# A two-role decoder step on eight cores: second-half cores split their columns 579 + 512, and 12 tokens change sides

## The reference, cut to what matters

```python
h = rmsnorm(x, g_pre1) * (1.0 + scale1) + shift1
z = h @ w_in                                  # 2048 -> 7168
u_pool, u_lru, g_pool, g_lru = split(z)       # 1024, 2048, 2048, 2048
y_pool = pool_mix(u_pool)                     # causal means over 2/4/8/16 tokens, then per-group maps
xc = causal_dwconv(u_lru, width 4)
y_lru = rglru(xc)                             # per-block gates, then a recurrence over the tokens
merged = sigmoid(g_pool) * (y_pool @ w_pool_up) + sigmoid(g_lru) * (y_lru @ w_lru_up)
x = x + gate1 * rmsnorm(merged @ w_out, g_post1)
h = rmsnorm(x, g_pre2) * (1.0 + scale2) + shift2
upc = causal_dwconv(h @ w_ffn_up, width 3)    # 2048 -> 2 x 6144
f = gelu(gt) * val                            # gt, val: the two parts of upc
x = x + gate2 * rmsnorm(f @ w_ffn_down, g_post2)
```

## Time and profile before

| | |
|---|---|
| runs, median | 2374.85 us (2374.43 to 2376.0, 3 runs) |
| the profiled execution | 2376.36 us |
| its slowest core, span from first to last instruction | 2374.8 us (core 1) |
| spans of all cores | 2292.6 to 2374.8 us |
| busy on core 1: PE / DVE / ACT / POOL | 90% / 44% / 38% / 6% |
| matmuls on core 1 | 17,232 |
| HBM read and written by core 1 | 585.81 MB, 21.32 MB |

### The profile page before, as it was taken

One profiled execution on the slowest core, in us unless ns is written; L12 is line 12 of the kernel. 1 busy time (PEld: TensorE's weight loads), 2 busy tenths in 40 slices (PEclk: granted clock), 3 DMA queues, 4 the chain that ended last, 5 costly groups with the idle time before them and its releaser, 6 DMA issues.

```text
span 2374.8 us, 42702 instructions; the slowest of 8 cores (2292.6 to 2374.8 us)
## 1 busy us (share of the span) xinstructions
PE 2147.8 (90%) x17232; PEld 1076.3 (45%) x17232; DVE 1033.4 (44%) x2122; ACT 899.6 (38%) x1232; POOL 146.5 (6%) x281
## 2 busy tenths in 40 slices
PE   0438988987899999999899999999999999999995
PEld 0124444443455545554345555555554555555552
DVE  0346888897411111110346656550005766553003
ACT  1547787886300000002364454440104444442101
POOL 0000000000000000000000000000000000000000
PEclk9969999999999999999999999999999999999998
DMA  7996575556365556569889988778788997788973
GB/s 170 254 210 107 85 119 90 112 93 125 58 113 110 108 108 113 99 100 181 204 162 196 185 143 142 139 139 172 135 132 154 212 180 135 139 142 187 193 135 94
DMA packets 64908, 336.83 MB, mean 142 GB/s; under 512 B 7360, under 2 KB 7872, under 8 KB 32192
## 3 DMA queue, kind: packets, MB, share of 16 engines
q0 software_dynamic: 39888, 273.17, 66.0%
q1 hardware_dynamic: 24816, 60.83, 7.9%
HBM read 585.81 MB, written 21.32 MB: 256 GB/s over the span
## 4 chain that ended last, share of the span: by engine, by line
PE 85%; ACT 5%; DVE 3%; DMA 2%; issue 2%; another core or an unknown queue 2%; SPq 0%; ACTq 0%; DVEq 0%; POOL 0%; POOLq 0%
PE ps_all L264 85%; ACT sb_R L241 4%; DVE sb_R L244 3%; DMA sb_R<-xp 1%; DMA sb_w<-w_in 1%; ACT L241 1%; DVE sb_R L247 1%; DMA sb_w<-w_ada 0%; SPq L279 0%; DVE sb_mod L254 0%; ACT sb_rstd L241 0%; ACT sb_wsm L241 0%; SPq L404 0%; ACTq L163 0%
## 5 line engine op out<-in xcount | busy, mean ns | idle before, releaser
L264 PE MATMUL ps_all<-sb_R,sb_w 128*128 128x512 bf16 (+4 forms) x14848 | 1976.4, 291 | 19.8 <-DMA sb_w<-w_in 13.2
L264 PEld LDWEIGHTS ps_all<-sb_R,sb_w 128*128 128x128 bf16 x14848 | 976.0, 96 | 1002.1 <-issue 36.3
L241 ACT ACTIVATE sb_R<-ps_all 128x128 f32<-128x128 f32 (+6 forms) x416 | 207.8, 532 | 634.4 <-PE ps_all L264 584.7
L247 DVE SCALAR_TENSOR_TENSOR sb_R<-sb_R,sb_cvec 128x423 f32<-128x423 f32 (+3 forms) x576 | 371.4, 692 | 32.7 <-ACT sb_R L241 21.8
L241 ACT ACTIVATE sb_R<-sb_R 128x551 f32<-128x551 f32 (+9 forms) x216 | 203.5, 963 | 89.9 <-DMA sb_R<-xp 50.1
L244 DVE TENSOR_TENSOR sb_R<-sb_R 128x552 bf16<-128x552 f32 (+9 forms) x148 | 161.5, 1091 | 162.7 <-ACT sb_R L241 148.4
L241 ACT ACTIVATE sb_wsm<-ps_all 128x552 bf16<-128x552 f32 (+1 forms) x64 | 40.4, 632 | 417.5 <-PE ps_all L264 417.2
L241 ACT ACTIVATE sb_R<-ps_all,sb_cvec 128x552 f32<-128x552 f32 (+4 forms) x184 | 166.4, 906 | 18.8 <-DVE sb_R L244 12.8
L244 DVE TENSOR_TENSOR sb_R<-sb_R,sb_mod 128x128 f32<-128x128 f32 x96 | 27.0, 291 | 292.0 <-ACT sb_R L241 288.2
L264 PE MATMUL ps_all<-sb_R,sb_ones 128*128 128x512 bf16 (+2 forms) x160 | 45.2, 403 | 114.1 <-ACT sb_R L241 114.0
L264 PE MATMUL ps_all<-sb_R,sb_wsm 128*128 128x512 bf16 (+2 forms) x432 | 88.5, 350 | 42.3 <-ACT sb_R L241 37.4
(11 more groups left out here) (48 smaller groups left out, 709.3 us busy)
## 6 DMA issues: line engine op xcount, KB each, us to landing
sb_w<-w_ffn_up POOLq DMA_DIRECT2D x96, 1024.0 KB, 10.9
sb_w<-w_ada POOLq DMA_DIRECT2D x48, 1024.0 KB, 13.1
sb_w<-w_ffn_down POOLq DMA_DIRECT2D x48, 1024.0 KB, 9.6
sb_w<-w_in POOLq DMA_DIRECT2D x36, 1024.0 KB, 10.2
sb_w<-w_out POOLq DMA_DIRECT2D x16, 1024.0 KB, 11.6
sb_R<-xm SPq DMA_DIRECT2D x4, 2206.0 KB, 58.6
sb_R<-xp SPq DMA_DIRECT2D x4, 2146.0 KB, 60.0
sb_w<-w_lru_up POOLq DMA_DIRECT2D x8, 1024.0 KB, 12.9
```

Of the source, the lines that this page charges most:

```text
L241: return self.P.op("act", lambda e: e.activation(out=out, in_=in_, func=func, **kw), after)
L247: return self.P.op("dve", lambda e: e.scalar_tensor_tensor(out=out, in0=in0, scalar=scalar, in1=in1, op0=op0, op1=op1), after)
L264: return self.P.op("pe", lambda e: e.matmul(out, lhsT=lhsT, rhs=rhs, start=start, stop=stop), after, signal)
```

## The change

The boundary between the two roles moves by 12 tokens: even cores own 1088 and have N = 1216 columns, odd cores own 960 and have N = 1091, and NP = 1085. On odd cores half B has exactly 512 columns and only one group, and half A has 579, groups of 512 and 67. Even cores have halves of 608 and 608. The longer rows need room: the buffer R grows by 704 bytes a partition, `invc` gives up its own 256 bytes and moves into the scale factors of the first normalization, which are dead by then; it is loaded in `pool_first`, and on even cores only. The merged tensor's place is now above the staging buffers instead of above half B's activations. The signal of a finished block in `ffn_down` moves from the second group's matmul to the last group's.

```diff
@@ -18,14 +18,14 @@
 ENGS = ("pe", "act", "dve", "pool", "sp")
 
 SEQ = 2048
-T0 = 1076
+T0 = 1088
 NSAMP = 128
 SEQS = 16
 TS = 8
 OWNS = (T0, SEQ - T0)
 NMAX = T0 + NSAMP
 NP = T0 - 3
-R_BYTES = 155392
+R_BYTES = 156096
 
 CV_GPRE1, CV_GPOST1, CV_GPRE2, CV_GPOST2 = 0, 16, 32, 48
 CV_PSCALE = 64
@@ -60,8 +60,8 @@
     N = NPR + NSAMP
     SN = (N + 1) // 2 * 2
     SNB = up64(2 * N) // 2
-    NA = (N + 1) // 2
-    NB = N - NA
+    NB = 512 if role else N // 2
+    NA = N - NB
     SB_ = (NA + 1) // 2 * 2
     SBB = up64(2 * NA) // 2
     SPF = (NP + 1) // 2 * 2
@@ -85,13 +85,13 @@
     O_PS = O_PU + 4 * 4 * PU
     O_GB = O_AG
     O_GB3 = O_YPOOL - 4 * SN
-    O_MERGED = O_U
     O_OA = 0
     O_OB = 16 * 4 * SB_
     O_H2A = up64(2 * 16 * 4 * SB_)
     O_H2B = O_H2A + 16 * 2 * SBB
     NXST = 6
     O_XST = O_H2B + 2 * 2 * SBB
+    O_MERGED = max(O_U, up64(O_XST + NXST * 4 * SB_))
     O_FLO = R_BYTES - 32 * 2 * SBB
     O_FHI = 0
     FU = 2 + max(NA, NPR - NA + 160)
@@ -107,7 +107,7 @@
     assert O_SQ + 2 * 2 * SNB <= R_BYTES and O_XCB + 4 * 2 * SNB <= R_BYTES
     assert O_MERGED + 16 * 2 * SNB <= R_BYTES
     assert O_DB + 2 * 2 * SNB <= O_GB3 and O_PS + 2 * 4 * PU <= R_BYTES
-    assert O_GB + 2 * 4 * SN <= O_GB3 and O_H2B + 16 * 2 * SBB <= O_MERGED
+    assert O_GB + 2 * 4 * SN <= O_GB3
     assert O_XST + NXST * 4 * SB_ <= O_H2B + 16 * 2 * SBB <= O_FLO
     assert O_X1ST + 2 * 4 * SB_ <= O_H2B and O_X1B + 16 * 4 * SB_ <= O_FLO
     assert O_FU0 + (2 * (FU + SB_) + 2 * FU + SB_) * 4 <= O_OB
@@ -359,7 +359,6 @@
             self.cvec = self.sb("cvec", [128, NV], F32)
             self.dv = self.sb("dv", [128, 4, 16], F32)
             self.mod = self.sb("mod", [128, 6, 16, 17], F32)
-            self.invc = self.sb("invc", [128, 4, 16], F32)
             self.sl = self.sb("sl", [128, DK, 17], BF16)
             self.hist_lru = self.sb("hist_lru", [128, 16, 3], F32)
             self.h_carry = self.sb("h_carry", [128, 16], F32)
@@ -368,6 +367,7 @@
             self.stl = self.sb("stl", [128, 16, SEQS, 3], F32)
             self.sth = self.sb("sth", [128, 16, SEQS], F32)
             mod0 = self.mod[:, 0].rearrange("p k j -> p (k j)")
+            self.invc = self.mod[:, 1].rearrange("p k j -> p (k j)")[:, 0:64].rearrange("p (g t) -> p g t", g=4)
             self.hist_pool = mod0[:, 0:120].rearrange("p (c t) -> p c t", c=8)
             self.h15 = mod0[:, 120:248].bitcast(BF16).rearrange("p (k t) -> p k t", k=16)
             self.hist_up = self.sth[:].rearrange("p c s -> p (c s)")[:, 0:192].rearrange("p (c t) -> p c t", t=2)
@@ -469,7 +469,6 @@
                 for q in range(4)]
         self.t_stl = self.ld(self.stl[:], self.st_lconv, "stl")
         self.t_sth = self.ld(self.sth[:], self.st_lh, "sth")
-        self.t_inv = self.ld(self.invc[:], self.invc_d, "invc")
         t_one = self.Vset(self.ones[:], 1.0)
         self.t_mod = [None] * 6
         ta = self.A(th, cT, AF.Tanh, scale=0.5, after=[t_c])
@@ -880,6 +879,7 @@
         y_pool = self.bfv(O_YPOOL, 8, SNB)
         self.y_pool = y_pool
         t_stp = self.ld(stp, self.st_pool, "stp", after=half_free)
+        t_inv = None if ROLE else self.ld(self.invc, self.invc_d, "invc", after=half_free)
         groups = [(0, 512), (512, 1024), (1024, N)]
         ring = Ring([0, 3])
         z = {}
@@ -957,7 +957,7 @@
                 dt += [t1, t2]
                 s_done[:] = [t1, t2]
                 if ROLE == 0:
-                    tf = self.Vtt(self.fix[:, c, :], src[:, m0:m0 + 16], self.invc[:, g, :], ALU.mult, t + [self.t_inv])
+                    tf = self.Vtt(self.fix[:, c, :], src[:, m0:m0 + 16], self.invc[:, g, :], ALU.mult, t + [t_inv])
                     t3 = self.Vtt(db[:, c, 0:16], self.fix[:, c, :], u[:, m0:m0 + 16], ALU.subtract, [tf, t1])
                     dt.append(t3)
                 h1 = self.A(self.hist_pool[:, ch, :], u[:, PR - 15:PR], AF.Copy, after=ev[c])
@@ -1074,7 +1074,7 @@
         halves = {
             "A": dict(c0=0, n=NA, npr=NA, groups=[(0, 512), (512, NA)], o=self.f32v(O_OA, 16, SB_),
                       h2=self.bfv(O_H2A, 16, SBB), halo=HALO, y0=0, t_g=[None] * DK, t_d=[None] * DK),
-            "B": dict(c0=NA, n=NB, npr=NPR - NA, groups=[(0, 512), (512, NB)], o=self.f32v(O_OB, 16, SB_),
+            "B": dict(c0=NA, n=NB, npr=NPR - NA, groups=[(0, 512), (512, NB)][:2 - ROLE], o=self.f32v(O_OB, 16, SB_),
                       h2=self.bfv(O_H2B, 16, SBB), halo=0, y0=NA - HALO, t_g=[None] * DK, t_d=[None] * DK),
         }
         f_lo = self.bfv(O_FLO, 32, SBB)
@@ -1330,7 +1330,7 @@
                             first, fin = kk == 0, kk == 47
                             for gi, (a0, a1) in enumerate(H["groups"]):
                                 dd = [wt, ft[kk]] + (self.bfree(bs[j], 2) if first and gi == 0 else [])
-                                sig = k == DK - 1 and gi == 1
+                                sig = k == DK - 1 and gi == len(H["groups"]) - 1
                                 t = self.MM(self.ap_ps(bs[j], a1 - a0, a0), wsl[:, k, j * 128:(j + 1) * 128],
                                             f_ap(kk)[:, a0:a1], first, fin, dd, sig)
                                 if sig:
```

## The result

The changed kernel takes 2340.1 and 2340.4 us, against 2374.4 to 2376.0 before: a ratio of 0.9853, 95% interval 0.9829 to 0.9877. It is faster by 1.5%, and 23 us slower than forecast. The profiled execution took 2340.07 us.

A forecast was written before the change was run, and what follows sets the result against it. TensorE's matmuls were taken to bound the slowest, odd cores: terms summing to -58.9 us took core 1 from 2374.8 to 2315.9, while +20.8 took even core 4 to 2316.9, hence 2317 us, range 2311 to 2331.

The forecast's parts named there:

- (a): Odd cores' second half loses its whole small matmul: 2,608 of 39 columns at 25.3 ns, 66.0 us off.
- (b): Odd cores' first-half small matmul grows from 40 to 67 columns, 25.3 to 30.7 ns: 14.1 us on.
- (c): Odd cores, third group of the main pass: 79 to 67 columns in 1,376 matmuls, 6.9 us off.
- (d): Odd cores, third group of the pass over earlier tokens: 49 to 61 columns in 336 matmuls, 1.0 us on.
- rival 2: FFN matmuls: without the small matmul between, each lone 512 shows its 96 ns weight load; 2566 us, chance 0.03.
- the cover of the finish: Odd cores' second up-projection: stored first-half blocks land in 12.7 us, within two steps of 6.9; no transfer cost charged.
- rival 1: Odd cores' second up-projection: transfers bind at 238 GB/s asked for, through weight tiles or the double buffer; 2321 to 2340 us, chance 0.15.
- The even cores: Wider halves and third groups, last stage and front add 20.8 us, taking core 4 from 2296.1 to 2316.9 us.
- (f): Odd cores' last stage: 16 VectorE operations shrink from 1.31 to 1.22 us each, 1.5 us off.
- (g): Odd cores, loading and normalizing: earlier tokens grow by 1.1%, main ones shrink; 0.7 us on, between 0 and 1.5.
- The sum without the stall: Slowest core is the larger of odd core 1's 2315.9 and even core 4's 2316.9 us, forecast as 2317.

## Why the prediction was wrong

- **Terms (a) to (d)** held: the lone 512, the 67 and the 61 columns measure 215.8, 30.7 to 30.9 and 28.4 ns. The rule of the Trainium skill ("TensorE: Matmul & The Clock Gate", "The mechanism") that weight loads overlap with matmuls in flight only when their row groups differ, and with it **rival 2**, does not hold for this kernel: a 512 behind a 512 with other weights costs 215.8 ns, so nothing of the 96 ns load shows. The prediction left out that the same section also lets a load into a background weight buffer be pulled ahead, which would agree.
- **The step that failed** is the cover of the finish: the sum charges nothing for transfers in the second up-projection, because "TensorE never waited" and 12.7 us to land fit two steps of 6.9, and rival 1 got 0.15. The runs showed in its place a stall of 22.2 us on core 3, out of the 25.0 by which it missed its forecast (33.9 us saved, 58.9 forecast). I had read the waits of core 1 alone, the slowest core, where VectorE waited 2.2 us for stored blocks. Cores 3 and 5 of the same execution, in the same stretch, show the cover already used up:

```profile
DVE sb_R L244 <- DMA sb_R<-x1s: 20.1, 7, 6.0
```

```profile
DVE sb_R L244 <- DMA sb_R<-x1s: 16.6, 7, 6.0
```

  It was 21.7 us on core 7. With three of four odd cores already losing up to 6.0 us at a time, 14% more bytes per us were unlikely to stay hidden, and rival 1 deserved far more than 0.15. Its own text named the place, the double buffer, and the time 2340 at its upper end; the other half of it, late weight tiles, didn't come: TensorE never waited for one. The second error was to hold a median of 12.7 us, again core 1's, against a deadline of 13.8. The same loads took 14.2, 14.1 and 13.5 us in the median on cores 3, 5 and 7 before, so two of the three medians were already past it, and the loads that stop an engine are the late ones, 18 and 21 us on core 3 after the change.
- **The price of the stall** was also cut short: a wait of TensorE of some 5 us costs its length and then a stretch at half clock, 4.5 us on top of 16.9 on core 3.
- **The even cores** were charged 20.8 us and took 12 to 17 more. 6 columns at 1.7 in place of 2.5 ns account for 5,216 x 0.8 = 4.2 us of that; the rest, 0 to 5 us, differs from core to core and was not traced.
- **Term (f)** was small: the 16 operations went from 1.31 to 1.22 or 1.23 us each as forecast, but the whole end behind the last squares only from 27.6 to 26.8 us on core 3, 0.8 off and not 1.5. **Terms (c), (d) and (g)** up to the end of the recurrent stage should have cancelled; core 3 got there 3.6 us later, the other odd cores 0.3 earlier to 1.9 later. What made the difference on core 3 was not tried.
- **The sum without the stall** came out, 2317 forecast and 2318 with half the pace, with some luck: 2317 was the even cores' sum, and there they took 2308 to 2311 us. The odd cores' own sum, 2315.9, is near their 2312 to 2315 in the profiled execution.

## What to carry to other kernels

When an edit shortens a step of TensorE, everything paced by that step speeds up with it: compare bytes asked for per us, and each buffered load's latest landings, with the new step, on every core and not only on the slowest. An engine that waits without harm before the change is cover that is already spent; look for such waits first. A matmul group at the floor of about 25 ns is worth removing whole, while making it narrower was worth nothing here (40 to 34 columns).

## What the runs showed of the hardware that was not expected

- The transfer engines' share of 1.00 or 1.01 goes with 205 GB/s (core 3 before), 217 (with a third buffer) or 235 (even cores stopped). It says that something is always under way, not that no more bytes could be moved.
- Core 1 has fewer waits than the other odd cores in the changed kernel (10.8 against 15.3 to 16.9 us) and far more when the even ones have stopped (17.7 and 28.0 against 0.5 at most).
- Waits of 4.9 and 6.6 us in the middle of dense work were followed by TensorE at half clock: 32 matmuls in 8.75 in place of 7.07 us, window means of 0.93 and 0.86. Waits of 0.62, 1.87 and 2.92 us in the same stretch were not.
